# Five blocks of ada_w moved from the first mixture of experts into the dense feed-forward stage

## What is computed

```
cs = jax.nn.silu(c)
for l in range(DEPTH):
    mod = (cs @ ada_w[l] + ada_b[l])[:, None, :]
    sh1, sc1, g1, sh2, sc2, g2 = jnp.split(mod, 6, axis=-1)
    h = rms_norm(x, norm1_g[l]) * (1.0 + sc1) + sh1
    ...

def swiglu(xn, w_gu, w_down):
    g, u = jnp.split(xn @ w_gu, 2, axis=-1)
    return (jax.nn.silu(g) * u) @ w_down
```

## Time and profile before

| | us |
|---|---|
| median of 3 runs | 3322.86 |
| lowest and highest run | 3321.74, 3334.63 |
| span of the profiled execution | 3321.5 |
| dense feed-forward stage, first gate/up to last down | 325.3 to 558.7 |
| first mixture, first gate/up to last scatter | 869.0 to 2128.0 |

### The profile page before, as it was taken

The page is one execution under the profiler, slowest core; times in us unless marked ns, Lnnn a source line. Parts: engine busy times, 40 slices in busy tenths (PEclk is TensorE's granted clock), DMA queues, the critical chain, the costliest instruction groups (busy, mean ns, idle before and its releaser), DMA issues. The chain is left out here.

```text
span 3321.5 us, 39376 instructions
## 1 busy us (share of the span) xinstructions
PE 3059.3 (92%) x17001; PEld 2459.8 (74%) x17003; DVE 802.0 (24%) x2027; ACT 396.6 (12%) x1042; POOL 53.8 (2%) x67
## 2 busy tenths in 40 slices
PE   3998999989799999999999999796799997997998
PEld 3767888758788888888787877574688777557876
DVE  1212112952211111111120000216323312562112
ACT  1102000011100000000000000104100000442001
POOL 0000000600000000000000000000000000000000
PEclk9999999999899999999999999997899995698999
DMA  7332455310687888788888786600258950004472
GB/s 238 121 127 101 159 193 193 127 51 0 256 329 285 317 308 318 285 312 314 301 300 327 280 305 251 253 26 0 88 188 302 349 141 0 1 1 133 161 239 91
DMA packets 328592, 645.26 MB, mean 194 GB/s; under 512 B 12875, under 2 KB 98273, under 8 KB 328417
## 3 DMA queue, kind: packets, MB, share of 16 engines
q1 hardware_dynamic: 318608, 636.51, 53.4%
q10 hardware_dynamic: 9809, 6.20, 0.7%
HBM read 641.64 MB, written 1.05 MB: 193 GB/s over the span
## 5 line engine op out<-in xcount | busy, mean ns | idle before, releaser
L1104 PEld LDWEIGHTS bank<-xn,ring 128*128 128x128 f32 x8896 | 1099.6, 192 | 65.7 <-issue 33.0
L1104 PE MATMUL bank<-xn,ring 128*128 128x128 f32 (+5 forms) x8896 | 1132.7, 289 | 7.3 <-issue 6.8
L997 PE MATMUL bank<-xn,ring 128*128 128x256 f32 x2048 | 462.7, 390 | 54.3 <-DVE xn L2390 17.7
L997 PEld LDWEIGHTS bank<-xn,ring 128*128 128x128 f32 x2048 | 400.8, 196 | 116.7 <-issue 41.1
L1133 PE MATMUL bank<-ring,att 128*128 128x512 f32 (+4 forms) x896 | 393.7, 594 | 0.0
L1985 DVE TENSOR_TENSOR att<-att,bank 128x128 f32<-128x128 f32 (+5 forms) x246 | 68.1, 278 | 1265.2 <-ACT att L1633 1265.2
L1133 PEld LDWEIGHTS bank<-ring,att 128*128 128x128 f32 (+4 forms) x896 | 149.2, 171 | 207.2 <-issue 206.8
L1633 ACT ACTIVATE att<-bank 128x128 f32<-128x128 f32 (+5 forms) x246 | 66.4, 270 | 1269.1 <-PE bank L1104 1269.1
L1280 PE MATMUL bank<-ring,att 128*128 128x512 f32 (+2 forms) x320 | 140.7, 595 | 0.0
L2022 DVE SCALAR_TENSOR_TENSOR sq<-ring,cs,sq 128x512 f32<-128x512 f32 x168 | 126.3, 752 | 6.0
L1104 PEld LDWEIGHTS bank<-sq,ring 128*128 128x128 f32 x1024 | 115.4, 192 | 4.8 <-issue 4.8
(11 more groups left out here) (249 smaller groups left out, 1974.9 us busy)
## 6 DMA issues: line engine op xcount, KB each, us to landing
ring<-od_moe_gu SPq DMA_DIRECT2D x112, 2048.0 KB, 13.1
ring<-od_moe_down SPq DMA_DIRECT2D x56, 2048.0 KB, 18.2
ring<-ada_w SPq DMA_DIRECT2D x24, 2048.0 KB, 17.0
ring<-moe_w_gate SPq DMA_DIRECT2D x32, 1024.0 KB, 13.9
ring<-moe_w_up SPq DMA_DIRECT2D x32, 1024.0 KB, 12.1
ring<-moe_w_down SPq DMA_DIRECT2D x16, 2048.0 KB, 14.3
ring<-ev_w_in SPq DMA_DIRECT2D x10, 2048.0 KB, 15.9
ring<-ev_ffn_gu SPq DMA_DIRECT2D x10, 2048.0 KB, 12.7
```

The source lines that it names most:

```text
L997: mm = nc.tensor.matmul(ps[:, c * T:(c + 1) * T], kblk(b)[:, k, u * T + c * P:u * T + (c + 1) * P], x[:, k, :], start=k == 0, stop=k == KD ...
L1104: mm = nc.tensor.matmul(ps[:, half * T:half * T + w], kblk(b)[:, k, j * P:(j + 1) * P], src[:, k, 0:w], start=k == 0, stop=k == KD - 1)
```

## The change

`ffn_steps` takes a further set of steps, `ada_twice`, in which a second ada block is made behind the down block. The dense stage gets it for steps 0 to 4, so a step's blocks there are gate, up, ada, down, ada, and 10 ada blocks are made in it. `ada_turn` takes any number of blocks, so both are summed by DVE at the end of their step, and PE has two sums to make in the next. The first mixture makes 7 in place of 12: experts 0 to 2 in steps 0 and 3, expert 3 in step 3 alone, the others none. The seven of the second block stay. Which block of `ada_w` is which doesn't change, nor what is done with it.

```diff
-        def ada_turn(x, a):
-
-            x.ada, x.ada_in = list(ada_left), [a] if a else []
+        def ada_turn(x, *made):
+
+            x.ada, x.ada_in = list(ada_left), [a for a in made if a]
             for given in x.ada:
                 given.fill = fill_turn()
             ada_left[:] = x.ada_in
 
-        def ffn_steps(n_hidden, gate_up, down, ada_at=(), after_first=None):
+        def ffn_steps(n_hidden, gate_up, down, ada_at=(), after_first=None, ada_twice=()):
...
                 x.gate, x.up = block(*g), block(*u)
                 a = ada_block() if s in ada_at else None
                 x.down = block(*down(s, x.n * P))
+                more = ada_block() if s in ada_twice else None
...
-                ada_turn(x, a)
+                ada_turn(x, a, more)
...
         ffn = ffn_steps(D_FF, ffn_load, lambda s, n: [row_load(A["ev_ffn_down"][0], s * HSTEP, n)],
-                        ada_at=range(D_FF // HSTEP))
+                        ada_at=range(D_FF // HSTEP), ada_twice=range(D_FF // HSTEP))
...
                            lambda s, n: [moe_row(s * HSTEP)], after_first=scatter_fills,
-                           ada_at=(0, 3) if i < 6 else ())
+                           ada_at=(0, 3) if i < 3 else (3,) if i < 4 else ())
```

## The result

The changed kernel took 3392.72 us (median of 4 runs, 3392.49 to 3392.83) against 3322.36 of the kernel before beside it (3321.74 to 3334.63): the ratio is 1.0218, interval 1.0187 to 1.0249, and the difference is +70.4 us. The forecast was 3379.6, +56.7 us. The time lies in the range given for 8 cases in 10 (3367 to 3399) and above the forecast's own range (3375 to 3386), so 13.7 us have to be accounted for. The profiled execution took 3392.66 us, its span 3390.9: 69.4 more than the span before.

A forecast was written before the change was run, and what follows sets the result against it. PE was taken as the bound of both stages. Waits of 40.2 and 8.1, clock restarts 8.8 and sums -0.4 gave +56.7 us on 3322.9: 3379.6 us, own range 3375 to 3386, 8 in 10 within 3367 to 3399.

The forecast's parts named there:

- What bounds the kernel: Dense stage and first mixture: PE is the bound, 92% busy; DVE's second sum stays covered at no cost.
- The slot of the down block: Dense stage: gate load of step s+1 takes the slot of step s-1's down block, giving four waits, steps 2 to 5.
- Rival A: Dense stage: gate load goes out before down starts, so its landing is hidden; no change, 3322.5 us; chance 4%.
- Rival B: Dense stage: five loads served together, so the pair lands with the last; +106 us, 3429 us; chance 5%.
- rival C: Dense stage: last wait falls away, or the clock doesn't fall in the gaps; 3369 to 3371 us; chance 8%.
- Rival D: Dense stage: a further unseen wait, for instance second ada block landing late; 12 to 28 us, 3392 to 3408; chance 9%.
- The price of a wait: Dense stage: 13.4 us for each of three waits, 40.2 in all, and 8.1 for the fourth, with 1 MB loads.
- The clock: Dense stage: PE restarts at 1.2 GHz after each wait, 2.2 us each, 8.8 for four, ends 6.4 and 10.4.
- The sums: Five ada sums more in the dense stage (+4.05 us), five fewer in the first mixture (-4.45): -0.4 us.
- What was forecast at nothing: Effects beyond the dense waits, restarts and sums: mixture's 6.80 us wait stays, shifted bank turn within half a us.
- What else is late next: Dense stage and mixture: later loads land in time, the mixture's first wait stays, no gain beyond the sums.
- the wide range: Whole kernel: 3367 to 3399 us, to hold 8 in 10, allowing for rivals and the scatter of runs upward.

The follow-up runs named there:

- the repeated run: Kernel before and changed kernel, both unaltered, run again on another chip: before 3318.49 us, changed 3382.38 us, ratio 1.0177.
- the dense part alone: Changed dense stage (10 ada blocks) with the first mixture left at 12, against the kernel before: 3366.95 us, ratio 1.0121.

## Why the prediction was right or wrong

**What bounds the kernel** held: PE is the bound of both stages, DVE's second sum and the extra 2 MB of a step cost nothing by themselves (with the down block one step later the stage is 4.28 us longer than before, PE's work on the sums alone).

**The slot of the down block** held in place and in number. Waits ahead of gate/up of steps 2, 3, 4 and 5 and nowhere else, the gate load 0.03 us after the end of down, and the wait gone, halved or single when the order of the blocks is altered. Rival A fell with the first trace; its argument, the low DMA share, was true and beside the point, as the late down block shows. Rival B fell by the landings (409.2, 419.7 and 425.1, where it wanted the pair at the end) and by the two prices, 8 us for one load in wait and 13.4 for two. Of rival C neither half came. Rival D, DVE late by the second ada block, didn't either: the block landed at 425.1, about 16 us into the group, and the dense stage has no wait beside the four.

**The price of a wait** held for the three: 13.60, 13.43 and 13.40 against 13.4. The fourth was forecast at 8.1 and measured 8.87, as its first load of 1 MB took 5.7 us to land and not 4.9; in two further traces it was 8.10 and 8.35. Waits in all 49.3 against 48.3. The image used for the price, a pair issued from an empty queue at the same moment of the step, was the right one.

**The clock:** forecast 8.8. In the trace after 2.35 + 1.79 + 1.51 + 1.93 = 7.6; by the same subtraction 9.6 in the repeated run and 10.7 in the run with the dense part alone. A restart after nearly the same idle time (13.4 to 13.7 us) took from 1.5 to 3.1 us, so the ends of 1.6 and 2.6 were too close for one restart; the ends for four (6.4 and 10.4) hold two of the three sums.

**The sums:** in the dense stage each took 0.89 us (1.70 to the next group in place of 0.81), not 0.81: 4.45, so the five there and the five in the mixture are even, and not -0.4. In the dense stage 49.3 + 7.6 + 4.5 = 61.4, which is what the boundaries show.

**What was forecast at nothing** is where it went wrong. The step that failed is "What else is late next", which looked for waits alone and put the rest of the kernel at nothing, within half a us. Against the forecast the stretch up to the mixture has +3.3, the mixture +1.3 (its one restart took 1.4 us more), and the last attention, 2200 us behind the dense stage, +9.25; the dense stage has +0.3 and the rest together -1.4. The work of the last attention is unchanged and its waits are no longer; the granted clock is what differs. The forecast carried this in the scatter of the runs, not as a term, so that the time still fell into the wide range owes something to luck: the room above the forecast was made for the scatter and rival D, and not for this.

How much of the 9.25 us belongs to the change is not settled. For it speaks that both kernels had their own length of the stage again in a second trace; against it, that the kernel with the same dense stage and twelve blocks in the mixture has the shortest. The medians don't settle it either: the repeated set gave +59.4 where the first gave +70.4, and the two pairs of profiled executions lie 69.4 and 71.3 us apart in their spans. With +59.4 the forecast is off by 2.7 us, with +70.4 by 13.7; the closeness of the first is no confirmation, as the one traced execution of that set has a dense stage 1.8 us over the forecast's and the long last attention too.

**What stays open:** what decides the clock of the last attention. Over the kernels it took 184.7, 191.2, 195.5, 200.1, about 205 and 215 us, with the records of PE the same but for one or two. It recurs to 0.03 us between two traces of one kernel on two chips, for both kernels that were traced twice, so in the profiled executions it isn't noise. It isn't moved by more than about 1 us by 0.85 or 1.7 us of shift, it isn't set by the waits of the dense stage, and it isn't set by the ada blocks of the second mixture alone. A large shift in time wasn't tried, and none of the executions that lie 13 us from the profiled one of their kernel has a trace.

## What to carry to other kernels

Where loads of different lifetimes share a ring, write down for each load whose slot it takes before adding a block to a step: at 5 blocks in a step and 7 slots the first load of a step took the slot freed last, and each step paid the landing time in full with the DMA engines busy for 0.48 of it (395.70 to 455.00 us). Asking for each block in the order in which slots come free removes the wait without a byte less, here 57 us by making the down load one step later. The slots alone don't make the total: with the wait gone the median was still 11 us over before. When totals differ by a few tenths of a per cent, compare stages by the same instruction in both traces: here gains and losses of 5 to 21 us came from the clock in a stage that no edit touched.

## What the runs showed of the hardware

- A narrow group that meets the clock at 1.2 GHz can stay there for its whole length with no idle time in it: 128 records of 60 columns took 27.40 us (granted clock 0.50 from end to end) in place of 15.16 (0.95), and 128 records of 64 columns 26.61 in place of 14.48. The second group of 60 columns, which follows behind 16 small records with 0.6 us of idle time between, took 25.7 to 27.6 us in all fourteen traces, also where the first had run in 14.5 to 15.2. A group of 256 columns after a gap of 13.4 us lost only 1.5 to 3.1 us. I had expected a restart to cost about the same anywhere.
- In two of the kernels that fall came after a wait of just 1.50 and 1.45 us ahead of the 64-wide group; after waits of 1.04 to 1.35 us, in eight other traces, the group took 14.47 or 14.48. No run tests whether the length of the wait decides it.
- Runs of one kernel lay up to 30 us apart (before: 3307.7 to 3337.1 on one chip), while the first mixture, the second and the last attention of that kernel recurred within 0.05 us between two traces. The stretches with restarts after long waits recurred less well: its dense stage 233.45 and 234.76 us, that of the changed kernel 294.86 and 297.74.
- Five loads of 2 MB on one queue landed in the order of issue, some 5 us apart and at up to 388 GB/s, even with SP taking 5.23 us to issue one of them.
